# A transformer kernel on one Trainium2 core: GpSimd splits ten more weight units, before and at the start of the sparse attention

## The chip, the core and the metric

The kernel runs on one core of one Trainium2 chip. The engines named here are TensorE (PE in the rows, its weight loads PEld), VectorE (DVE), ScalarE (ACT), GpSimd (POOL) and SyncE (SP, which issues the weight loads). The metric is the device time of one execution in microseconds (us), lower is better. A time is the median of several runs; a profile is one further execution.

## What is computed

The reference is two blocks in fp32 on 256 tokens of width 1024: a first model of two layers (Fourier and window attention, pooling, SwiGLU), and a second block that this change touches. The second block ("third block" in the kernel's own counting, since the first model has two) is, cut to what matters:

```python
h = rmsnorm(x, norm_mix)
(dn_qkv, dn_z, dn_b, dn_a, ns_q, ns_kc, ns_vc, ns_ks, ns_vs, ns_kw, ns_vw, ns_gate,
 gate_dn, gate_nsa) = jnp.split(h @ w_in, splits, axis=-1)
o_dn = gated_deltanet(dn_qkv, dn_z, dn_b, dn_a, ...)
o_ns = nsa_mixer(ns_q, ns_kc, ..., ns_gate, ...)   # compressed, selected and window attention
mix = sigmoid(gate_dn) * (o_dn @ w_proj_dn) + sigmoid(gate_nsa) * (o_ns @ w_proj_nsa)
x = x + mix @ w_out
x = x + square(relu(rmsnorm(x, norm_mlp) @ w_up)) @ w_down
```

The products ns_q, ns_ks, ns_kw and the raw keys and values ns_kc, ns_vc stand first (stage f1 of the kernel), then the token-major values ns_vs, ns_vw (tm1), then dn_qkv (stage f2), beside which the sparse attention runs.

## The kernel before

Every weight product is made of three matmuls of reduced-precision fp32: a weight unit of 128x1024 floats is split into a high part (sb_whi, the rounded copy) and a low part (sb_wlo, weight minus high part), and lines 578 to 580 multiply high by high, high by low and low by high. A unit serves one tile of 128 output features and 24 matmuls. Four pairs of buffers hold split units, so unit n takes the buffers of unit n-4: whoever splits unit n waits until PE has finished unit n-4 and until the unit's chunk has landed (SP loads chunks of two units into ring slots, and reuses a slot when the low parts of its old chunk are done).

Who splits is set by one tuple, POOLED (line 319). For a unit outside it, ACT makes the high part (line 1456) and DVE the low part (line 2039), each at the place in its own queue that the planner `Flow` gives, up to three units ahead of PE's use. For a unit in POOLED, GpSimd makes both parts (lines 2866 and 2868), and PE waits for GpSimd's semaphore s_lo_pool in place of s_lo_dve. Before the change POOLED holds ten units of f2: numbers +5, +7 to +23 counted from f2's first unit.

Counted like that, the units of the stage in question are: -21 to -18, raw keys and values (tiles j = 12 to 15); -17, half a unit, the gates; -16 to -5, queries and keys j = 0 to 11; -4 to -1, values (`values2`); from 0 on, f2. PE runs them in this order, with small products between them. After every odd j from 1 on, `f1_squares(j)` (line 597) sums squares, ACT takes a root (line 1731), DVE inverts it and spreads it over heads (`f1_inverse(j)`, lines 2374 and 2376, the latter a copy of 128x512 within SBUF into sb_tmp), PE turns that (`f1_spread(j)`, line 1031), and DVE scales the tiles with it (`unit_rms(j)`, line 2384). Between them stand the compressed keys and values: DVE writes sb_bk in `blocks(e)` (line 2411, eight tensor-tensor instructions on 64 partitions, two SBUF inputs), PE multiplies it by raw weights (line 1056), DVE and ACT apply a gelu (lines 2417 to 2427, 1764), and PE scores against the result (`cmp_scores`, line 1088), which needs the tiles of `unit_rms(7)`.

No scheduler orders any of this: each engine's queue is the order in which its program function writes it, and engines meet only at semaphores. GpSimd's queue before the change, in this part, is three memsets, then a wait for the end of f1 on PE, ACT and DVE, then per attention step a multiplication of the scores (`weigh`, line 2859) and for every second step a split.

Of the kernel before, what the change touches and what calls it, by code (L numbers as in the profile page):

```python
# [9 lines left out]
ALU = mybir.AluOpType  # L10
# [305 lines left out]

F2 = (*range(8, 16), *range(8), *range(16, 24))
F2_UNIT = FIRST_UNIT[[name for name, _, _, _ in PLAN].index("f2")]
POOLED = tuple(F2_UNIT + s for s in range(5, 24, 2))
ADDED = {"ffn1": 4}  # L320
CUTS = ((0, 128), (128, 384))
NORMS = ("mix0", "ctx", "ffn0", "mix1", "ffn1", "fin", "mix2", "mlp2")
# [9 lines left out]
def program(nc, a):  # L332
    ctx = ExitStack()
    with ctx:
        area = [ctx]

        def sb(name, shape, dt=F32):
            return area[-1].enter_context(nc.sbuf_tensor("sb_" + name, shape, dt))
# [5 lines left out]
        def sem(name):  # L344
            return ctx.enter_context(nc.semaphore(name))
# [12 lines left out]
        pe, act, dve, pool = Mark(sem("s_pe")), Mark(sem("s_act")), Mark(sem("s_dve")), Mark(sem("s_pool"))  # L358
# [100 lines left out]
        ss = sb("ss", [128, 3, 2, 384])  # L459
        pt2 = sb("pt2", [128, 2, 2, 384])  # L460
        nst = st[:, 0:64].rearrange("p (n k u t) -> p n k u t", n=4, k=4, u=2)
# [51 lines left out]
        def landed(c):  # L513
            return s_slot[SLOT_OF[c]], 16 * LOADS[c]

        def unit_of(n):
            c, o, size = UNITS[n]
            return chunk(c)[:, o:o + size], whi[:, n % NUNIT, 0:size], wlo[:, n % NUNIT, 0:size]

        def lo_done(n):  # L520
            return lo_pool.at(n) if n in POOLED else lo_dve.at(n)

# [913 lines left out]
        def scalar_program(sc):  # L1436
# [10 lines left out]
            def split(units):  # L1447

                for n in units:
                    if n in POOLED:  # L1450
                        continue
# [569 lines left out]
        def vector_program(ve):  # L2021
# [10 lines left out]
            def split(units):  # L2032

                for n in units:
                    if n in POOLED:
                        continue
# [762 lines left out]
        def gpsimd_program(gp):  # L2799
            G = Waiter(gp)  # L2800

            def regions(before):

                G.wait_ge(*pe.at(before))
                G.wait_ge(*act.at(before))
                G.wait_ge(*dve.at(before))
# [42 lines left out]
            gp.memset(hvx[:, :, :, :], 0.0).then_inc(*pool.up("hvx"))  # L2849
            gp.memset(bk[:, :, :], 0.0).then_inc(*pool.up("bk"))  # L2850
            gp.memset(pcs[:, :, :, :], 0.0).then_inc(*pool.up("pcs"))
            pool.note("f1")
            regions("f1")
            def weigh(i):
                G.wait_ge(*dve.at("nw", i))
                for t, (lo, hi) in enumerate(CUTS):
                    p = ss[:, i % 3, :, lo:hi]
                    x = nst[:, i % 4, 3, :, t].unsqueeze(2).to_broadcast([128, 2, hi - lo])
                    gp.tensor_tensor(p, p, x, ALU.mult).then_inc(*pool.up(*[("weighed", i)] * t))  # L2859

            def split(n):

                x, hi, lo = unit_of(n)
                G.wait_ge(*landed(UNITS[n][0]))
                G.wait_ge(*pe.at("unit", n - NUNIT))
                gp.tensor_copy(hi, x).then_inc(*pool.up(("hi", n)))
                G.wait_ge(*pool.at("hi", n))
                gp.tensor_tensor(lo, x, hi.bitcast(F32), ALU.subtract).then_inc(*lo_pool.up(n))

            weigh(0)  # L2870
            step = 2
            for s in range(24):
                if STEPS2[s]:
                    if step - 1 < N2:
                        weigh(step - 1)
                    step += 1
                if F2_UNIT + s + AHEAD in POOLED:
                    split(F2_UNIT + s + AHEAD)
# [33 lines left out]
        def sync_program(sp):  # L2912
# [31 lines left out]
            for c in range(len(PLAN)):  # L2944
                if c == 4:
                    sp.dma_start(h[:, :, :], a["xT"]).then_inc(s_x, 16)
                if c == 10:
# [4 lines left out]

        engines = ((tensor_program, nc.tensor), (scalar_program, nc.scalar), (vector_program, nc.vector),
                   (gpsimd_program, nc.gpsimd), (sync_program, nc.sync))
        marks = (pe, act, dve, pool, hi_done, lo_dve, lo_pool)
        for walk, _ in engines:
# [22 lines left out]
        @block.gpsimd  # L2979
        def _(eng):  # L2980
            gpsimd_program(eng)
# [206 lines left out]
```

## Time and profile before

| | us |
|---|---|
| median of 3 runs | 1146.68 (1144.14 to 1146.83) |
| the profiled execution, own time | 1141.37 |
| its span from first to last instruction | 1139.6 |
| PE busy | 1109.6 |
| DVE busy | 812.3 |
| ACT busy | 586.5 |
| POOL busy | 135.4 |

The span is 1.8 us shorter than the execution's own time; what lies around it is not in the trace. PE's busy time is modelled at the ends of matmuls, so small gaps in PE are best read from the list of waits. A wait is written as "who waited, its line <- whose result, its line". In the timeline a row is one or several like instructions, with start, duration, engine, line, operation, and in brackets how long the engine had been idle and what ended that.

### The profile page before, as it was taken

What the parts mean: (1) busy time and instruction counts of PE and PEld (TensorE: products, weight loads), DVE (VectorE), ACT (ScalarE), POOL (GpSimd) and SP (SyncE); (2) the same over time, 40 slices, a digit from 0 to 9 for tenths busy, and PEclk for the clock granted to TensorE, in tenths of its full rate; (3) what the DMA queues carried; (4) which work ended last, traced back from release to release, by engine and by line L of the source; (5) the groups of instructions that cost most, each with busy time, mean ns of one, the idle gap of its engine ahead of it and who ended that gap; (6) DMA issues with size and microseconds to landing.
All of it is one profiled execution on the core that took longest, in us unless ns stands there. A gap on an engine that the chain in (4) does not pass through costs nothing.

```text
span 1139.6 us, 23794 instructions
## 1 busy us (share of the span) xinstructions
PE 1109.6 (97%) x10111; PEld 1049.6 (92%) x10111; DVE 812.3 (71%) x1436; ACT 586.5 (51%) x1081; POOL 135.4 (12%) x143
## 2 busy tenths in 40 slices
PE   8899999999999999999999999999999999999998
PEld 2786889999998999999988888889989999999998
DVE  6887889898887766554766787778545667677553
ACT  2546654545445544554556677653325556565342
POOL 0002100000111000012000365525300002000000
PEclk9899999999999999999999999999999999999999
DMA  9965299898883676540752332322025555755610
GB/s 389 388 249 181 79 365 359 324 337 334 315 344 112 246 279 240 193 163 8 290 185 80 144 112 82 122 94 76 4 74 185 185 186 210 308 188 187 225 55 15
DMA packets 32221, 225.36 MB, mean 198 GB/s; under 512 B 3569, under 2 KB 4721, under 8 KB 5105
## 3 DMA queue, kind: packets, MB, share of 16 engines
q1 hardware_dynamic: 30530, 221.21, 52.0%
q10 hardware_dynamic: 1584, 2.62, 0.7%
q8 instruction: 80, 1.31, 0.5%
q14 instruction: 27, 0.22, 0.1%
HBM read 222.76 MB, written 1.05 MB: 196 GB/s over the span
## 4 chain that ended last, share of the span: by engine, by line
PE 89%; DVE 6%; ACT 3%; DMA 1%; issue 1%; POOL 0%; DVEq 0%; ACTq 0%; POOLq 0%
PE bank L578 24%; PE bank L579 23%; PE bank L580 23%; DVE sb_wlo L2039 2%; PE bank L597 1%; DMA sb_ring<-in_ada 1%; PE bank L1110 1%; PE bank L1141 1%; ACT sb_whi L1456 1%; PE bank L1119 1%; PE bank L1306 1%; PE bank L1324 1%; PE bank L1320 1%; PE bank L673 1%; PE bank L678 1%; PE bank L674 1%
## 5 line engine op out<-in xcount | busy, mean ns | idle before, releaser
L578 PE MATMUL bank<-sb_xh,sb_whi 128*128 128x256 f32 x1480 | 416.7, 282 | 2.5 <-DVE sb_wlo L2039 2.2
L580 PE MATMUL bank<-sb_xh,sb_wlo 128*128 128x256 f32 x1480 | 409.4, 277 | 0.0
L579 PE MATMUL bank<-sb_xl,sb_whi 128*128 128x256 f32 x1480 | 409.4, 277 | 0.0
L2039 DVE TENSOR_TENSOR sb_wlo<-sb_ring,sb_whi 128x1024 fp32r<-128x1024 f32 (+1 forms) x185 | 229.7, 1247 | 103.4 <-ACT sb_whi L1456 103.0
L578 PEld LDWEIGHTS bank<-sb_xh,sb_whi 128*128 128x128 f32 x1480 | 277.7, 188 | 9.5 <-issue 5.6
L579 PEld LDWEIGHTS bank<-sb_xl,sb_whi 128*128 128x128 f32 x1480 | 277.7, 188 | 0.1
L580 PEld LDWEIGHTS bank<-sb_xh,sb_wlo 128*128 128x128 f32 x1480 | 277.5, 188 | 0.0
L1456 ACT ACTIVATE sb_whi<-sb_ring 128x1024 fp32r<-128x1024 f32 (+1 forms) x185 | 194.3, 1054 | 96.7 <-PE bank L580 81.8
L2039 DVE TENSOR_TENSOR sb_wlo<-sb_more,sb_whi 128x1024 fp32r<-128x1024 f32 x110 | 133.9, 1228 | 62.7 <-ACT sb_whi L1456 62.7
L578 PE MATMUL bank<-sb_hh,sb_whi 128*128 128x256 f32 x608 | 168.4, 277 | 0.0
L579 PE MATMUL bank<-sb_hl,sb_whi 128*128 128x256 f32 x608 | 167.8, 276 | 0.0
L580 PE MATMUL bank<-sb_hh,sb_wlo 128*128 128x256 f32 x608 | 167.8, 276 | 0.0
L1456 ACT ACTIVATE sb_whi<-sb_more 128x1024 fp32r<-128x1024 f32 x110 | 116.1, 1058 | 65.8 <-PE bank L580 53.8
L579 PEld LDWEIGHTS bank<-sb_hl,sb_whi 128*128 128x128 f32 x608 | 114.2, 188 | 0.0
L578 PEld LDWEIGHTS bank<-sb_hh,sb_whi 128*128 128x128 f32 x608 | 114.1, 188 | 0.0
L580 PEld LDWEIGHTS bank<-sb_hh,sb_wlo 128*128 128x128 f32 x608 | 114.1, 188 | 0.0
L2814 POOL TENSOR_TENSOR sb_sq<-sb_sq 128x256 f32<-128x256 f32 x22 | 23.9, 1088 | 347.4 <-ACT sb_sq L1478 209.7
L2083 DVE CUSTOM_DVE_ANT_0 sb_ring<-sb_ring,sb_cB,sb_col 128x1024 f32<-128x1024 f32 x44 | 55.6, 1299 | 0.0
L1649 ACT ACTIVATE sb_tmp<-bank 128x256 f32<-128x256 f32 x44 | 16.9, 384 | 66.2 <-PE bank L580 66.2
L2083 DVE CUSTOM_DVE_ANT_0 sb_more<-sb_more,sb_cB,sb_col 128x1024 f32<-128x1024 f32 x36 | 45.4, 1297 | 0.0
L2859 POOL TENSOR_TENSOR sb_ss<-sb_ss,sb_st 128x256 f32<-128x256 f32 (+1 forms) x32 | 26.9, 863 | 134.2 <-DVE sb_st L2507 133.8
L1478 ACT ACTIVATE sb_sq<-sb_h 128x256 f32<-128x256 f32 x40 | 15.8, 414 | 48.4 <-DVE sb_h L2097 43.9
(411 smaller groups left out, 1848.3 us busy)
## 6 DMA issues: line engine op xcount, KB each, us to landing
sb_more<-in_w SPq DMA_DIRECT2D x34, 1024.0 KB, 6.0
sb_ring<-in_w SPq DMA_DIRECT2D x32, 1024.0 KB, 5.9
sb_ring<-in_adaT SPq DMA_DIRECT2D x24, 1024.0 KB, 7.1
sb_ring<-in_f SPq DMA_DIRECT2D x22, 1024.0 KB, 4.9
sb_more<-in_adaT SPq DMA_DIRECT2D x20, 1024.0 KB, 8.5
sb_ring<-in_gn SPq DMA_DIRECT2D x8, 1024.0 KB, 4.8
sb_ring<-in_gd SPq DMA_DIRECT2D x8, 1024.0 KB, 5.0
sb_ring<-in_up SPq DMA_DIRECT2D x8, 1024.0 KB, 8.1
```

Source lines behind the costliest of these rows:

```text
L578: te.matmul(out, wh, rh, start=start, stop=False, skip_group_check=skip)
L579: te.matmul(out, wh, rl, start=False, stop=False, skip_group_check=skip)
L580: return te.matmul(out, wl, rh, start=False, stop=stop, skip_group_check=skip)
L597: end = te.matmul(out(t), src[:, c + t * 128:c + (t + 1) * 128], ones_, start=True, stop=True)
L673: te.matmul(out, hi[:, c], xh[:, k, :], start=clear and k == 0, stop=False, skip_group_check=True)
L1456: sc.activation(hi, x, ACT.Copy).then_inc(*hi_done.up(n))
L1478: sc.activation(sq[:, k, :], src[:, k, :], ACT.Square).then_inc(*act.up(("sq", norm, k)))
L1649: sc.activation(temp(("silu", layer, j), (dve, ("hid", layer, j))), ps_of(("up", layer, j))[:, 0:T], ACT.Silu).then_inc(*act.up(("silu", l ...
L2039: ve.tensor_tensor(lo, x, hi.bitcast(F32), ALU.subtract).then_inc(*lo_dve.up(n))
L2083: ve.tensor_tensor_reduce(out=x, in0=x, in1=cB[:, 0, :], scale=1.0, scalar=C(f"ab{layer}", jj, jj + 1), op0=ALU.mult, op1=ALU.add, accum_o ...
L2814: gp.tensor_tensor(sq[:, 0, :], sq[:, 0, :], sq[:, k, :], ALU.add).then_inc(*pool.up(("sum", norm, k)))
L2859: gp.tensor_tensor(p, p, x, ALU.mult).then_inc(*pool.up(*[("weighed", i)] * t))
```

## The change

POOLED begins 20 numbers earlier: it now holds -15, -13, -11, -9, -7, -5, -3, -1, +1, +3 too, every second unit from there to +23. GpSimd's `split` moves up and is called for the eight units below zero right behind the memsets, ahead of the wait for the end of f1; the split of +1 stands behind that wait and ahead of weigh(0), that of +3 ahead of weigh(1). ACT and DVE each have ten instructions fewer.

```diff
-POOLED = tuple(F2_UNIT + s for s in range(5, 24, 2))
+POOLED = tuple(F2_UNIT + s for s in range(-15, 24, 2))
...
+            def split(n):
+
+                x, hi, lo = unit_of(n)
+                G.wait_ge(*landed(UNITS[n][0]))
+                G.wait_ge(*pe.at("unit", n - NUNIT))
+                gp.tensor_copy(hi, x).then_inc(*pool.up(("hi", n)))
+                G.wait_ge(*pool.at("hi", n))
+                gp.tensor_tensor(lo, x, hi.bitcast(F32), ALU.subtract).then_inc(*lo_pool.up(n))
+
             pool.note("f1")
+            for n in range(F2_UNIT - 15, F2_UNIT, 2):
+                split(n)
             regions("f1")
...
+            split(F2_UNIT + 1)
             weigh(0)
```

GpSimd's queue behind the three memsets, before the change (2859 is weigh, 2866 and 2868 are a split):

```order
L2851 MEMSET sb_pc 128x1024
L2859 TENSOR_TENSOR sb_ss<-sb_ss,sb_st 128x2x128 [waits s_dve,s_act,s_pe]
L2859 TENSOR_TENSOR sb_ss<-sb_ss,sb_st 128x2x256
L2859 TENSOR_TENSOR sb_ss<-sb_ss,sb_st 128x2x128 [waits s_dve]
L2859 TENSOR_TENSOR sb_ss<-sb_ss,sb_st 128x2x256
```

The same place after it (2857 and 2859 are now the split, 2870 is weigh); two of the eight early splits and the last ones before weigh(0):

```order
L2851 MEMSET sb_pc 128x1024
L2857 CAST sb_whi<-sb_ring 128x1024 [waits s_pe,s_slot2]
L2859 TENSOR_TENSOR sb_wlo<-sb_ring,sb_whi 128x1024 [waits s_pool]
L2857 CAST sb_whi<-sb_qk 128x1024 [waits s_pe,s_slot4]
L2859 TENSOR_TENSOR sb_wlo<-sb_qk,sb_whi 128x1024 [waits s_pool]
...
L2857 CAST sb_whi<-sb_ring 128x1024 [waits s_slot2,s_dve,s_pe,s_act]
L2859 TENSOR_TENSOR sb_wlo<-sb_ring,sb_whi 128x1024 [waits s_pool]
L2870 TENSOR_TENSOR sb_ss<-sb_ss,sb_st 128x2x128 [waits s_dve]
```

Eight splits now wait only for PE's progress and the loads, and the ninth (unit +1) has taken over the wait for f1 and stands ahead of weigh(0).

DVE's queue at the start of the stage before the change: the splits of -16, -15, -14 and -13, then blocks(0) (2411), gates (2342 to 2347), the split of -12 and the first head scale (2374, 2376):

```order
L2039 TENSOR_TENSOR sb_wlo<-sb_ring,sb_whi 128x1024 [waits s_hi]
L2337 SCALAR_TENSOR_TENSOR sb_h<-sb_h,sb_col,bank 128x256 x2
L2039 TENSOR_TENSOR sb_wlo<-sb_ring,sb_whi 128x1024 [waits s_hi]
L2337 SCALAR_TENSOR_TENSOR sb_h<-sb_h,sb_col,bank 128x256 x2
L2039 TENSOR_TENSOR sb_wlo<-sb_qk,sb_whi 128x1024 [waits s_hi] x2
L2411 TENSOR_TENSOR sb_bk<-sb_kcv,sb_col 64x16x15 [waits s_act,s_pool]
L2411 TENSOR_TENSOR sb_bk<-sb_kcv,sb_col 64x16x15 x7
```

And after it:

```order
L2039 TENSOR_TENSOR sb_wlo<-sb_ring,sb_whi 128x1024 [waits s_hi]
L2337 SCALAR_TENSOR_TENSOR sb_h<-sb_h,sb_col,bank 128x256 x4
L2039 TENSOR_TENSOR sb_wlo<-sb_qk,sb_whi 128x1024 [waits s_hi]
L2411 TENSOR_TENSOR sb_bk<-sb_kcv,sb_col 64x16x15 [waits s_act,s_pool]
L2411 TENSOR_TENSOR sb_bk<-sb_kcv,sb_col 64x16x15 x7
```

The splits of -15 and -13 have left DVE's queue, and blocks(0) follows the split of -14 with nothing between.

## Rows read from the trace of the kernel before

**Rows 1.** The page: busy us, share and instructions of each engine

```profile
PE 1109.6 (97%) x10111; PEld 1049.6 (92%) x10111; DVE 812.3 (71%) x1436; ACT 586.5 (51%) x1081; POOL 135.4 (12%) x143
```

**Rows 2.** PE's waits, 540 to 760 us: total us, times, longest

```profile
PE bank L597 <- DVE sb_nq L2384: 1.4, 1, 1.4
PE bank L1031 <- DVE sb_tmp L2376: 1.3, 2, 0.9
PE bank L1088 <- DVE sb_hdev L2374: 0.9, 1, 0.9
...
PE bank L578 <- ACT sb_vsw L1812: 0.3, 1, 0.3
```

**Rows 3.** GpSimd's two split instructions: ns minimum/median/maximum, first and last start

```profile
L2866 POOL CAST sb_whi<-sb_ring x10: 1037/1238/1287, 645.7 to 734.1; 128x1024 fp32r<-128x1024 f32 x10
...
L2868 POOL TENSOR_TENSOR sb_wlo<-sb_ring,sb_whi x10: 2357/2372/2446, 647.0 to 735.5; 128x1024 fp32r<-128x1024 f32 x10
```

**Rows 4.** Timeline, GpSimd and DVE beside each other, f2 and behind it

```profile
647.01 2.40 POOL L2868 TENSOR_TENSOR sb_wlo<-sb_ring,sb_whi 128x1024 fp32r<-128x1024 f32 x1
648.64 1.85 DVE L2039 TENSOR_TENSOR sb_wlo<-sb_ring,sb_whi 128x1024 fp32r<-128x1024 f32 x1 [1.06 <-ACT sb_whi L1456]
...
652.37 0.17 DVE L2507 TENSOR_TENSOR sb_st<-sb_st,sb_gate 128x4 f32<-128x4 f32 x1
655.49 2.37 POOL L2868 TENSOR_TENSOR sb_wlo<-sb_ring,sb_whi 128x1024 fp32r<-128x1024 f32 x1
656.19 1.69 DVE L2507 TENSOR_TENSOR sb_st<-sb_st,sb_gate 128x4 f32<-128x4 f32 x1
...
660.26 1.29 POOL L2866 CAST sb_whi<-sb_ring 128x1024 fp32r<-128x1024 f32 x1 [0.69 <-PE bank L580]
660.58 1.25 DVE L2583 SCALAR_TENSOR_TENSOR sb_qk<-sb_tmp,sb_qk 128x256 f32<-128x256 f32 x1
...
759.62 0.34 DVE L2640 TENSOR_SCALAR sb_Msb<-sb_con,sb_gg 128x256 f32<-128x256 f32 x1
759.73 1.09 POOL L2885 TENSOR_TENSOR sb_Msb<-sb_Msb,sb_con 128x384 f32<-128x384 f32 x1 [15.45 <-ACT sb_Msb L1927]
759.88 1.02 DVE L2641 TENSOR_SCALAR sb_Msb<-sb_con,sb_gg 128x128 f32<-128x128 f32 x1
```

**Rows 5.** Timeline, start of the queries: ACT, DVE, PE, 558 to 571 us

```profile
558.32 0.38 ACT L1711 ACTIVATE sb_tmp<-bank 64x256 f32<-64x256 f32 x1 [0.44 <-PE bank L580]
...
558.89 1.22 DVE L2039 TENSOR_TENSOR sb_wlo<-sb_qk,sb_whi 128x1024 fp32r<-128x1024 f32 x1
...
562.68 1.23 DVE L2039 TENSOR_TENSOR sb_wlo<-sb_qk,sb_whi 128x1024 fp32r<-128x1024 f32 x1 [2.58 <-ACT sb_whi L1456]
563.82 4.09 DVE L2411 TENSOR_TENSOR sb_bk<-sb_kcv,sb_col 64x240 f32<-64x240 f32 x8
...
569.93 0.43 DVE L2376 COPY sb_tmp<-sb_hdev 128x512 f32<-128x512 f32 x1
...
570.47 0.60 PE L1031 MATMUL bank<-sb_con,sb_tmp 128*128 128x128 f32 x4
```

**Rows 6.** Timeline, end of f1 and the values: PE, DVE, ACT, 602 to 634 us

```profile
602.49 0.60 PE L1031 MATMUL bank<-sb_con,sb_tmp 128*128 128x128 f32 x4
...
605.32 1.23 DVE L2039 TENSOR_TENSOR sb_wlo<-sb_ring,sb_whi 128x1024 fp32r<-128x1024 f32 x1 [1.05 <-ACT sb_whi L1456]
...
612.21 0.60 PE L1031 MATMUL bank<-sb_con,sb_tmp 128*128 128x128 f32 x4
...
614.05 1.23 DVE L2039 TENSOR_TENSOR sb_wlo<-sb_ring,sb_whi 128x1024 fp32r<-128x1024 f32 x1 [2.67 <-ACT sb_whi L1456]
...
626.77 0.25 DVE L2481 TENSOR_TENSOR sb_cst<-sb_cst,sb_gate 128x8 f32<-128x8 f32 x2
...
633.17 0.66 ACT L1812 ACTIVATE sb_vsw<-bank 128x256 f32<-128x256 f32 x2 [0.59 <-PE bank L580]
```

**Rows 7.** PE by 2 us stretches: length, PE busy (instructions), granted clock, DMA share, GB/s

```profile
618.00:620.00 2.00, 1.61 (x8) 0.50 0.00 0
```

More of the change, by code:

```diff
@@ L2859, in weigh @@
                     gp.tensor_tensor(p, p, x, ALU.mult).then_inc(*pool.up(*[("weighed", i)] * t))
[L2861 to L2868, printed above, removed]
+            split(F2_UNIT + 1)
             weigh(0)
```

## The prediction

> **What bounds the kernel now.** The page first: PE is busy for 1109.6 of 1139.6 us [rows 1], so nothing that makes DVE or ACT idle more is worth anything unless PE waits for it. The list of PE's waits for the stretch of the change comes next. From 540 to 760 us the waits that end in this part's work are four kinds [rows 2]: 1.4 us at line 597 for the bank that unit_rms(3) frees, 1.3 us in two waits at line 1031 for the head scale of line 2376 (0.9 the longer), 0.9 us at line 1088 for unit_rms(7) (its second instruction ends just ahead of the one named), and 0.3 us at line 578 for ACT's copy of the values. That is 3.9 us in all, and it is the ceiling of what relief can give before any clock is counted. PE never waits there for a split. In f2 itself, where GpSimd splits already, no row of the list names DVE or ACT work behind a split, so the four later places decide.
>
> **What the relief is worth.** Ten ACT and ten DVE instructions go, about 1.05 and 1.22 us each. Only those on the way to one of the four waits count. Unit -9's low part stands ahead of the gelu that leads to the 1.4 us wait: 1.1 us off it. Unit -5's parts stand ahead of the second gelu, which leads through ACT's split of -4 to the 0.9 us wait; the next limit on that way (ACT must wait for PE's tile j = 9) is about 0.95 us earlier than now, so this wait would go. The other places (0.5, 0.9 and 0.3 us) hang on work that stays. Relief alone: about -2.0 us.
>
> **What a GpSimd split costs.** A cast of 1.04 to 1.29 us and a subtraction of 2.36 to 2.45 us [rows 3], 3.5 us with the gap, against one in 5.6 us of PE's time. GpSimd has nothing else to do there. PE's own need of these units is covered: unit n's buffers are free three units (8 us and more) before it is wanted, and 3.5 us is less. Unit -15 is wanted at 561.2, and its buffers are free three units before, near 552.8 [rows 5]. The loads are issued when low parts are done, and those come earlier, not later. weigh(0), now behind the split of +1, moves by a few us, and PE turns its scores only two attention steps later. All of that costs nothing.
>
> **What the split does to DVE.** In [rows 4] DVE's subtraction of line 2507, 128x4, takes 0.17 us at 652.37 and 1.69 us at 656.19; the second ends at 657.88, where GpSimd's subtraction of 655.49 ends (657.86). Line 2039 begins at 648.64 under a GpSimd subtraction that ends at 649.41, and ends 1.22 us after about 649.27. So a DVE instruction with two SBUF inputs does not run beside GpSimd's; it waits for its end. A fast one-input operation within SBUF does as well: line 2641 takes 1.02 us at 759.88 beside GpSimd's 759.73. Who comes next is seen there too: DVE's 2640 runs to 759.96, 2641 is queued right behind it, and GpSimd, which asked at 759.73, gets in between. So does the cast of 660.26 ahead of DVE's 2583, which begins at 660.58 and ends at 661.83, 0.28 us behind the cast. I take it that they alternate: each lets the other's waiting instruction go after its own current one.
>
> The Trainium skill has this as a rule (SBUF — State Buffer, section "Who interferes with whom"): the pair of ports that DVE and GpSimd share is an exclusive lock held for the whole instruction, and a DVE instruction with two SBUF inputs contends with a GpSimd one that reads SBUF. The rows agree to 0.1 us. A reader who takes instead the mean lengthening of line 2039's rows (some 0.5 us on 1.22) as a slowdown in proportion gets the second rival below.
>
> **Term 1, the start.** On the clock of before [rows 5]. PE ends the gates' unit -17 at 558.2 (ACT takes it at 558.32) and j = 3, unit -13, at 570.5, where line 1031 starts. Between them are four units of 2.8 us and 1.1 us of small work, so -15 ends at 564.0. Hence the casts of -13, -11 and -9 are released at 558.3, 564.1 and 570.6. DVE reaches the split of -14 at 558.7, waits for the cast of -13 (559.4) and ends it at 560.6. GpSimd's subtraction then holds DVE until 562.9, where blocks(0) starts; that is 0.9 us earlier than now (563.82). Two or three of its eight instructions (0.51 us each) pass by 564.4, then the cast of -11 (to 565.4), one more, then its subtraction (565.9 to 568.3), then the rest: blocks(0) ends at 570.4 and not at 567.9. From its end to that of line 2376 it is 2.45 us now (567.91 to 570.36), with two small two-input instructions and one of line 2039. The cast of -9 is released at 570.6, and its subtraction ends at 574.2; the split of -12 comes behind it, then 2374 and 2376: 576.1. PE wants it at 570.5. The stall is 5.6 us. If DVE kept the port through a run of queued instructions, I get 573.3, a stall of 2.7 us; if they shared it freely, none. I take 5.6, since the rows at 660.26 and 759.73 show GpSimd getting in.
>
> **Term 2, the first gelu.** After the stall blocks(1) runs with GpSimd idle. The 0.5 us wait at the second line 1031 goes. The gelu and the split of -8 meet the split of -7 (released when j = 5 ends), and the wait at line 597 stays at about 1.3 us in place of 0.3. Net -0.5 us.
>
> **Term 3, unit_rms(7).** [Rows 6], again on the clock of before: -3's split is released when j = 9 ends, at 602.5, and holds until 606.2. ACT's high part of -4 would let line 2039 start 0.95 us earlier, at 604.4; it gets the port at 606.15 and not at 605.32 as now. +0.85 us at line 1088.
>
> **Term 4, head scale 11.** Unit -1's split runs from 612.4 (j = 11 ended at 612.2) to 616.0. Line 2039 for -2, at 614.05 now, starts at 615.9, and everything to line 2376 and PE follows: +1.85 us.
>
> **Term 5, the values.** Unit +1's split runs from 626.1 to 629.6. It holds line 2481 at 626.77 and what follows; the scores of pair 1 and their exponentials come 2.5 us late. ACT has one cast less (1.0 us) and idles 0.6 us ahead of its copy at 633.17, so PE's first f2 unit waits 0.9 us longer.
>
> **Clock.** Behind the present stall at 618 the granted clock is 0.50 for a stretch of 2 us [rows 7], the lower level of 1.2 GHz; the engine had done little but small matmuls and waits before. A stall of 5.6 us at 570.5 should bring the same: 2 us at half speed lose 1.0 us; bounds 0 and 2.
>
> Sum: 5.6 - 0.5 + 0.85 + 1.85 + 0.9 + 1.0 = +9.7 us. The profiled execution took 1141.37 us, of which 1139.6 are span, so one like it would take 1151.1; the median of the runs is 1146.68, 5.3 above it, and becomes **1156.4**.
>
> **The rivals.**
> *GpSimd gets in less (2.7 in place of 5.6, no clock loss):* 2.7 - 0.5 + 0.85 + 1.85 + 0.9 = +5.8, 1152.5. For it: a run of eight queued instructions is not in the rows.
> *Slowed in proportion:* each DVE instruction that meets a split loses some 0.5 us. Four or five of them before 570.5 eat 2.3 us of the 3.3 us by which blocks(0) could start earlier (563.82 against 560.6), and no stall appears; later four meetings on the way to waits cost 2.0 and the relief gives 2.0: 0, 1146.7. Against it: 1.69 us for 128x4 elements.
> *Relief wins, not slower:* if the 64-partition instructions of line 2411 pass beside GpSimd, blocks(0) ends near 565, line 2376 at 568 at the latest, and the later meetings fall into DVE's idle time: -2.0, 1144.7. It decides at one point, whether line 2376 is done by 570.5. For it: DVE is idle for 2.58 us ahead of 562.68. To be faster by more, the clock loss at 618 would have to go too (another 1 to 1.4 us with its wait), which hangs on ACT's and DVE's split of -2, and those stay.
> *The change doesn't do what it says:* GpSimd held by a late load, and PE waiting for s_lo_pool. The cover is 4.5 us, so this is small, and it counts with the slower ones.
>
> **Chances.** Forecast 0.50, less getting in 0.15, late splits 0.02: slower by over 0.3% 0.67. Proportion 0.14 and relief 0.14: within 0.3% (3.4 us, about what a measurement of this kernel tells from no change) 0.28. Faster by more 0.05. The range starts at relief's value, less 0.2, and ends 3.6 above the forecast, for a clock loss of 2 and another 2.6 us where ties between the engines fall badly: 1144.5 to 1160. Below it lies some 0.1, above some 0.1.
>
> **What would show it.** In the profile after: PE's first line 1031 in f1 waits for line 2376 by about 5.6 us (2.7 in the first rival, 0 in the others); DVE's line 2411 x8 takes 7 to 8 us and not 4.09; small two-input DVE instructions of 1 to 2 us beside GpSimd's subtraction; the waits at 1088 and at the last 1031 near 1.7 and 2.7 us; granted clock of 0.5 behind the first stall. If line 2411 still takes 4.1 us with a GpSimd split over it, term 1 falls, and the time is near 1145.

## The result and the profile after

The changed kernel takes **1152.7 us** (median of 8 runs, 1146.29 to 1155.0) against 1146.76 for the kernel before (8 runs, 1143.75 to 1147.41): a ratio of 1.0049, 95% interval 1.0025 to 1.0073, or 3 to 8 us slower. The forecast was 1156.4, the range 1144.5 to 1160. The same kernel in a later comparison gave 1.0035 (1.0013 to 1.0057), so +4 to +6 us is what the change costs. The profiled execution took 1151.45 us.

The head of its page: the span, then busy time, share and instructions of each engine ([rows 1] before).

```profile
span 1149.7 us, 23806 instructions
PE 1115.7 (97%) x10111; PEld 1054.8 (92%) x10111; DVE 820.6 (71%) x1426; ACT 577.2 (50%) x1071; POOL 172.7 (15%) x163
```

Ten instructions left DVE, some 12 us of work, and DVE is busy for 8.3 us longer than before. Its instructions wait inside their own duration. The page's group of line 2039 (count, busy us and mean ns, then the idle time ahead) shows it; before, the mean was 1247 ns over 185 instructions.

```profile
L2039 DVE TENSOR_TENSOR sb_wlo<-sb_ring,sb_whi 128x1024 fp32r<-128x1024 f32 (+1 forms) x177 | 230.0, 1304 | 105.9 <-ACT sb_whi L1456 105.5
```

PE's waits of the changed kernel, 540 to 775 us: who waited for whom, total us, times, longest ([rows 2] before).

```profile
PE bank L1269 <- DVE sb_Msb L2641: 2.1, 1, 2.1
PE bank L1031 <- DVE sb_tmp L2376: 1.9, 1, 1.9
PE bank L1110 <- DVE sb_pc L2462: 1.7, 1, 1.7
PE bank L1088 <- DVE sb_hdev L2374: 1.7, 1, 1.7
PE bank L597 <- DVE sb_nq L2384: 1.5, 1, 1.5
PE bank L578 <- ACT sb_vsw L1812: 1.4, 1, 1.4
PE bank L1073 <- ACT sb_hx L1768: 0.3, 1, 0.3
...
```

Without the first row, which lies at 760 us, and the 0.2 of line 673, which is there before and after, they come to 8.5 us. Before they were 4.5 (the 3.9 of [rows 2], and 0.3 us each at lines 606 and 1073). No wait for s_lo_pool is among them: GpSimd's splits are never late.

The rest of the difference between these two profiles is TensorE's clock. PE by stretches, the changed kernel: length, PE busy (instructions), granted clock, DMA share, GB/s.

```profile
536.00:544.00 8.00, 7.43 (x54) 1.00 0.58 213
584.00:596.00 12.00, 10.16 (x104) 0.86 0.07 18
604.00:616.00 12.00, 10.31 (x80) 0.72 0.25 87
616.00:628.00 12.00, 10.12 (x89) 0.85 0.25 89
756.00:772.00 16.00, 13.90 (x96) 0.89 0.26 95
```

The same stretches of the kernel before:

```profile
536.00:544.00 8.00, 7.51 (x40) 0.79 0.46 169
584.00:596.00 12.00, 10.33 (x119) 1.00 0.34 106
604.00:616.00 12.00, 11.14 (x129) 1.00 0.46 167
616.00:628.00 12.00, 11.12 (x84) 0.86 0.16 48
756.00:772.00 16.00, 14.25 (x103) 1.00 0.19 67
```

A granted clock of 0.86 over 12 us is a stretch at 0.50, the level of 1.2 GHz, that loses 12 x 0.14 = 1.7 us. Five such losses stand against two, 8.6 us against 3.4: +5.2. With +4.0 of waits and +0.4 at line 1269 that is 9.6 of the 10.1 us between the spans (1149.7 and 1139.6). Only the waits can be laid to the change at once. The profiled execution of before was quicker than each of its 8 runs (5.4 us under their median), that of after is 1.3 under its own median, so a part of the 5.2 us is the luck of two executions. How large that part is, the clocks of all runs show (the table under "Which units are worth it").

### The profile page after: what moved, and what is told of

It reads as the page before. It is cut to its first block, busy times and chain, and to the rows that moved or that the text cites. A ratio compares the mean times of both kernels' runs of the same rounds, so it can differ in the third digit from the quotient of the medians.

```text
span 1149.7 us, 23806 instructions
## 1 busy us (share of the span) xinstructions
PE 1115.7 (97%) x10111; PEld 1054.8 (92%) x10111; DVE 820.6 (71%) x1426; ACT 577.2 (50%) x1071; POOL 172.7 (15%) x163
## 3 DMA queue, kind: packets, MB, share of 16 engines
HBM read 222.76 MB, written 1.05 MB: 195 GB/s over the span
## 4 chain that ended last, share of the span: by engine, by line
PE 88%; DVE 8%; ACT 3%; issue 1%; POOL 0%; DMA 0%; ACTq 0%; DVEq 0%; POOLq 0%
PE bank L578 23%; PE bank L580 22%; PE bank L579 22%; DVE sb_wlo L2039 3%; PE bank L702 1%; PE bank L597 1%; PE bank L1141 1%; PE bank L1110 1%; ACT sb_whi L1456 1%; PE bank L1119 1%; PE bank L1306 1%; PE bank L1324 1%; PE bank L1320 1%; PE bank L673 1%; DVE sb_bk L2411 1%; PE bank L678 1%
## 5 line engine op out<-in xcount | busy, mean ns | idle before, releaser
L1456 ACT ACTIVATE sb_whi<-sb_ring 128x1024 fp32r<-128x1024 f32 (+1 forms) x177 | 185.9, 1053 | 96.4 <-PE bank L580 82.4
L2859 POOL TENSOR_TENSOR sb_wlo<-sb_ring,sb_whi 128x1024 fp32r<-128x1024 f32 x18 | 44.4, 2469 | 1.4
```

Source lines behind the costliest of these rows:

```text
L1456: sc.activation(hi, x, ACT.Copy).then_inc(*hi_done.up(n))
```

## The experiments

All are compared with the kernel before in 5 rounds. The forecast's theory, called the port theory in the expectations, is that GpSimd's reads hold DVE, and that DVE's lateness reaches PE. Against it stand three others: that GpSimd's splits come late, that the clock alone costs, or that any added work on GpSimd does. In each version GpSimd's calls of `split` follow the tuple.

### One half of the change at a time

Only the eight units below zero:

```diff
-POOLED = tuple(F2_UNIT + s for s in range(5, 24, 2))
+POOLED = tuple(F2_UNIT + s for s in (-15, -13, -11, -9, -7, -5, -3, -1, *range(5, 24, 2)))
```

> The changed kernel with +1 and +3 given back to ACT and DVE; GpSimd keeps the eight splits of -15 to -1. Port theory: the waits of PE before the values stay as in the changed kernel (line 1031 about 1.9, line 597 about 1.5, line 1088 about 1.7, line 1110 about 1.7 us), the wait for ACT's copy of the values falls from 1.4 back to 0.3 us; time 1.1 us below the changed kernel's 1152.7, about 1151.5. Rival, late splits (what costs is that weigh(0) and f2 stand behind +1 and +3): most of the 6 us go, 1147.

Measured: 1147.25 against 1144.59, ratio 1.0032 (1.0014 to 1.005). The rival's 1147 is met in microseconds, but only because the kernel before ran 2.2 us quicker in this comparison; as a ratio the rival says 1.000 and the port theory 1.004, and the measured one rules the first out. The waits are those of the changed kernel, without the one for the values (0.3 at line 578), with 0.5 in place of 1.7 at line 1110, which was not expected, and with the 0.3 at line 606 that the kernel before has too.

The other two units, +1 and +3:

```diff
-POOLED = tuple(F2_UNIT + s for s in range(5, 24, 2))
+POOLED = tuple(F2_UNIT + s for s in range(1, 24, 2))
```

> The kernel before with only +1 and +3 added to GpSimd; nothing in f1 changes. Port theory: PE's wait at line 578 for ACT's copy of the values grows from 0.3 to 1.2 to 1.4 us, f1's waits stay at 3.6 us in all; time 1147.7 (+1.0, within the noise of the kernel before). Rival, late splits: +4 to +6, 1151 to 1153.

Measured: 1145.9, ratio 1.0008 (0.9988 to 1.0027), as the port theory had it. In the list of waits the one at line 578 for ACT's copy is 1.4 us as in the changed kernel (0.3 before); the 0.3 at line 606 is gone, and the others are those of before to 0.1 us. So these two splits make the wait for the values, 1.1 us, and the early eight make all the others.

The 0.5 us at line 1110 in the first of these runs is a lesson in reading. Its timeline, PE and DVE:

```profile
615.38 0.60 PE L1031 MATMUL bank<-sb_con,sb_tmp 128*128 128x128 f32 x4
...
619.04 1.95 PE L1078 MATMUL bank<-sb_col,sb_hvx 128*128 128x64 f32 x8
...
620.93 0.46 DVE L2462 TENSOR_TENSOR sb_pc<-bank,sb_con 128x120 f32<-128x120 f32 x2
...
621.54 1.65 PE L1110 MATMUL bank<-sb_ksw,sb_nq 64*128 64x128 f32 x8 [0.55 <-DVE sb_pc L2462]
```

and that of the changed kernel:

```profile
616.93 0.60 PE L1031 MATMUL bank<-sb_con,sb_tmp 128*128 128x128 f32 x4
...
618.34 2.35 POOL L2859 TENSOR_TENSOR sb_wlo<-sb_ring,sb_whi 128x1024 fp32r<-128x1024 f32 x1
618.76 3.01 DVE L2039 TENSOR_TENSOR sb_wlo<-sb_ring,sb_whi 128x1024 fp32r<-128x1024 f32 x1 [4.58 <-ACT sb_whi L1456]
620.26 1.08 PE L1078 MATMUL bank<-sb_col,sb_hvx 128*128 128x64 f32 x8
...
623.08 1.66 PE L1110 MATMUL bank<-sb_ksw,sb_nq 64*128 64x128 f32 x8 [1.74 <-DVE sb_pc L2462]
...
624.40 0.43 DVE L2376 COPY sb_tmp<-sb_hdev 128x512 f32<-128x512 f32 x1
...
624.89 1.12 PE L1031 MATMUL bank<-sb_con,sb_tmp 128*128 128x128 f32 x4
```

and PE of the kernel before, behind the 612.21 of [rows 6]:

```profile
616.59 0.93 PE L1110 MATMUL bank<-sb_ksw,sb_nq 64*128 64x128 f32 x8
...
618.39 1.12 PE L1031 MATMUL bank<-sb_con,sb_tmp 128*128 128x128 f32 x4 [0.88 <-DVE sb_tmp L2376]
```

From line 1031 to line 1110 it is 6.2 us in both of the first (4.38 before). In the first, PE ran line 1078 in 1.95 us, at a granted clock of 0.50 (619 to 621 us); in the changed kernel it takes 1.08 at 1.00 (620 to 622 us). Its slow matmuls filled the wait (the rest of the difference is line 597, 1.38 us for 1.05). The changed kernel does the same one step on: line 1110 takes 1.66 us there (0.51 granted from 623 to 625 us) and 0.93 before, and line 1031 follows line 2376 without a wait, while the whole way from line 1031 to the next line 1031 has grown from 6.18 to 7.96 us. DVE sets these times; the list of waits shows only what PE has left of them.

### Is it the reading, or the work?

GpSimd is given as much work at the same places, but writes only: four memsets of the same buffers, 3.4 us. The split of these ten units is left out, and constants stand in for their weights. So PE multiplies other numbers; whether that touches its clock is not shown, but DVE's durations below do not hang on it.

```diff
+                if n < F2_UNIT + 5:
+                    gp.memset(hi.bitcast(F32), 0.03125).then_inc(*pool.up(("hi", n)))
+                    G.wait_ge(*pool.at("hi", n))
+                    gp.memset(lo.bitcast(F32), 0.0).then_inc(*pool.up())
...
+                    gp.memset(lo.bitcast(F32)[:, 0:512], 0.0).then_inc(*pool.up())
...
+                    gp.memset(lo.bitcast(F32), 0.0).then_inc(*lo_pool.up(n))
+                    return
```

> The changed kernel, but for the ten added units GpSimd fills the high and low parts with constants (memsets of about the same length, 0.95 and 2.4 us) and reads no weight, so these products are of constants; ACT and DVE are relieved as in the changed kernel. Port theory (it is GpSimd's reading of SBUF that holds DVE's two-input instructions): line 2411 x8 back to 4.1 us, PE's first wait at 1031 gone, the waits at 597 and 1088 at 0.3 and 0 us, time 1144.7, up to 3.4 lower by clock stretches that go, 1141 to 1146. Rival (GpSimd's length, its place in the chain of semaphores or any GpSimd access is what costs): 1150 to 1153 as the changed kernel.

The other way round: the kernel before, with ACT and DVE splitting all, and GpSimd reading beside them. It copies and subtracts at the eight early places, and nobody uses what it writes. (It writes as well as reads; that writing costs nothing is what the first of the two runs tests.)

```diff
+            for n in range(F2_UNIT - 15, F2_UNIT, 2):
+                x, y = flat(xh[:, 0:4, :]).bitcast(F32), flat(sq[:, 4:8, :])
...
+                G.wait_ge(*landed(UNITS[n][0]))
+                G.wait_ge(*pe.at("unit", n - NUNIT))
+                gp.tensor_copy(y, x).then_inc(*pool.up(("x", n)))
+                G.wait_ge(*pool.at("x", n))
+                gp.tensor_tensor(y, x, y, ALU.subtract).then_inc(*pool.up(("y", n)))
```

> The kernel before, all splits where they were, but GpSimd also runs eight pairs of a copy and a two-input subtraction of 128x1024 (activations read, a free part of sb_sq written, nobody uses it), released as the splits of -15 to -1 are in the changed kernel. Port theory: the cost without the relief, so more than the changed kernel: 2 us more waiting, +8 (6 to 12), 1152 to 1158, line 2411 x8 at 7 to 9 us. Rival (moving the splits away from ACT and DVE, or PE's waits for GpSimd's semaphore, is what costs): same as before, 1146.8.

Measured: writes only 1140.9, ratio 0.9973 (0.9958 to 0.9989); reads only 1154.13, ratio 1.0095 (1.007 to 1.012). The longest waits of the first:

```profile
PE bank L597 <- DVE sb_nq L2384: 0.7, 1, 0.7
PE bank L1031 <- DVE sb_hx L2417: 0.4, 1, 0.4
```

and of the second:

```profile
PE bank L1031 <- DVE sb_tmp L2376: 5.7, 2, 5.5
PE bank L1088 <- DVE sb_hdev L2374: 2.2, 1, 2.2
PE bank L1110 <- DVE sb_pc L2462: 1.8, 1, 1.8
```

One DVE group tells the two apart at its source, the eight two-input instructions of line 2411. In the timeline of writes only it takes what it took before ([rows 5], 4.09 us), with GpSimd writing beside it (one memset of four is shown; they run from 556.68 to 560.25):

```profile
556.52 4.10 DVE L2411 TENSOR_TENSOR sb_bk<-sb_kcv,sb_col 64x240 f32<-64x240 f32 x8
```

```profile
557.69 0.96 POOL L2860 MEMSET sb_wlo<- 128x1024 f32 x1
```

With reads only it takes 6.88 us (7 to 9 expected):

```profile
562.44 6.88 DVE L2411 TENSOR_TENSOR sb_bk<-sb_kcv,sb_col 64x240 f32<-64x240 f32 x8
```

So the reads cost, not the work: the relief alone is worth 3.1 us, the reads alone cost 10.9. The two do not add up to the change's 5.6: the first covers ten units and the second eight, and DVE stands elsewhere when GpSimd asks. The Trainium skill (SBUF — State Buffer, section "Who interferes with whom") says that a DVE instruction with two SBUF inputs contends with a GpSimd one that reads SBUF and not with one that only writes it; 4.10 beside the memsets and 6.88 beside the copies agree.

### Shorter turns

The ten added splits in four pieces each, 128x256:

```diff
+                if n < F2_UNIT + 5:
+                    for q in range(4):
+                        c = slice(q * 256, (q + 1) * 256)
+                        gp.tensor_copy(hi[:, c], x[:, c]).then_inc(*pool.up(*[("hi", n)] * (q == 3)))
...
+                        end = gp.tensor_tensor(lo[:, c], x[:, c], hi[:, c].bitcast(F32), ALU.subtract)
...
```

> The changed kernel, each of the ten added casts and subtractions in four pieces of 128x256. GpSimd's work grows (about 0.3 and 0.7 us a piece, 4 us a split), but no piece holds the port for more than 0.7 us. Port theory, with turns taken after each instruction: a DVE instruction waits for one piece and not for a whole subtraction, so the waits at 597, 1088, 1110 fall to some 0.7, 1.1 and 1.0 us, the first at 1031 stays between 0 and 2; ratio to before about 1.001 (0.999 to 1.003) against the changed kernel's 1.0049. Rival (the port is divided by time share, so the total GpSimd time counts, not the length of a piece): 1.005 or more.

Measured: 1147.12 against 1145.65, ratio 1.0013 (0.9998 to 1.0028). The groups of the pieces (count, busy us and mean ns):

```profile
L2864 POOL TENSOR_TENSOR sb_wlo<-sb_ring,sb_whi 128x256 fp32r<-128x256 f32 x32 | 28.5, 921 | 0.6
L2860 POOL CAST sb_whi<-sb_ring 128x256 fp32r<-128x256 f32 x32 | 13.4, 459 | 36.2 <-PE bank L580 36.2
```

A split costs GpSimd 4 x (0.92 + 0.46) = 5.5 us in place of 3.5, and yet PE's waits fall from 8.5 to 2.6 us, since a DVE instruction now waits for a turn of about 0.9 us and not for 2.4. The eight of line 2411 show it (ns, minimum, median and longest, of one), here and in the changed kernel:

```profile
L2411 DVE TENSOR_TENSOR sb_bk<-sb_kcv,sb_col x8: 579/820/1033, 556.8 to 562.0; 64x240 f32<-64x240 f32 x8
```

```profile
L2411 DVE TENSOR_TENSOR sb_bk<-sb_kcv,sb_col x8: 558/564/2687, 558.0 to 566.4; 64x240 f32<-64x240 f32 x8
```

The lock is handed over at instructions. The time does not fall as far as the waits. In this profile the clock accounts for that: 0.93 granted between 540 and 640 us, where the kernel before has 0.97, so 4 us lost. Over all runs it accounts for little (+0.7 us in the table below), and why the time stays at that of before with 1.9 us less waiting isn't shown.

### Which units are worth it

If relief counts only where a unit stands ahead of a wait, a few units should do, and those that hold DVE should be left.

```diff
-POOLED = tuple(F2_UNIT + s for s in range(5, 24, 2))
+POOLED = tuple(F2_UNIT + s for s in (-9, -5, *range(5, 24, 2)))
```

> The kernel before, with only units -9 and -5 added to GpSimd: the two whose DVE part stands ahead of a gelu that PE waits for, and whose GpSimd split runs while DVE has slack. Port theory: wait at 597 from 1.4 to 0.7 or less, at 1088 from 0.9 to 0, the others as before; ratio 0.9985 (0.997 to 1.000). Rival (any split on GpSimd in f1 costs): 1.001 or more.

The same with `(-9, -4, -2, *range(5, 24, 2))`:

> The kernel before, with -9, -4 and -2 added to GpSimd: the last two are the units whose split stands right ahead of unit_rms(7) and unit_rms(9) on DVE. Port theory: waits at 597 0.7 or less, at 1088 0, at the last 1031 (head scale 11) 0 in place of 0.9, a new one of up to 0.3 at 1031 for head scale 7 (GpSimd's subtraction of -4 runs until 602.3 on the clock of before); with the low-clock stretch at 618 gone too, ratio 0.996 (0.9945 to 0.999). Rival (any split on GpSimd in f1 costs): 1.001 or more.

The changed kernel without -13 and -11, `(-15, -9, -7, -5, -3, -1, *range(1, 24, 2))`, to test the first stall alone:

> The changed kernel with -13 and -11 given back to ACT and DVE, so that no GpSimd split runs over blocks(0). Port theory: line 2411 x8 back to 4.1 us, PE's first wait at 1031 (1.9 us) gone, the waits at 597, 1088, 1110 and 578 stay at 1.5, 1.7, 1.7 and 1.4; ratio 1.003 (1.0015 to 1.005). Rival (the stall at 1031 comes from the backlog of earlier splits, not from the overlap with line 2411): the 1.9 us stay, 1.005.

Measured: 0.9964 (0.9951 to 0.9978) with -9 and -5, quicker than the whole range expected; 0.9959 (0.9944 to 0.9973) with -9, -4 and -2; 1.0041 (1.0026 to 1.0057) without -13 and -11. In the last, line 2411 takes its 4.13 us again and the first wait for line 2376 is gone; 0.7 us for line 2417 and 0.9 for line 2427, the gelus behind it, come in its place. Line 1110 waits 0.6 us and not the 1.7 expected; here too line 1078 runs in 1.95 us and fills it. The first stall is therefore not what the time hangs on.

Then both picks together, and the changed kernel beside it once more:

```diff
-POOLED = tuple(F2_UNIT + s for s in range(5, 24, 2))
+POOLED = tuple(F2_UNIT + s for s in (-9, -5, -4, -2, *range(5, 24, 2)))
```

> The kernel before with -9, -5, -4 and -2 added to GpSimd, the two selections that were faster together. Both take the wait at 1088 away already (0.9 us), so only -5's part ahead of the second gelu could still give something, and that wait is gone: port theory expects no gain over -9, -4, -2 alone, ratio 0.996 (0.9945 to 0.9975). Rival (each unit taken off ACT and DVE is worth its share, some 0.2% for two): 0.994.

> The changed kernel once more, on the chip and in the rounds of this job. PE's six waits of the stretch come back to 0.1 us (1.9 at 1031, 1.5 at 597, 1.7 at 1088, 1.7 at 1110, 1.4 at 578, 2.1 or 1.7 at 1269), since they follow from order and durations alone. If the number of stretches at the low clock is a matter of chance, it differs from the first profile's (588, 608 to 616, 620 to 627, 764 us) and the time with it, 1.7 us a stretch; ratio 1.005 (1.003 to 1.008).

Measured: **1138.47** against 1144.66, ratio 0.9948 (0.9929 to 0.9968), the fastest version; the changed kernel 1147.61, ratio 1.0035. Three units gave 0.9959, so what the fourth adds isn't told apart; the rival's 0.994 lies within the interval too. PE's waits with four units:

```profile
PE bank L1031 <- DVE sb_hx L2417: 0.9, 2, 0.7
PE bank L597 <- DVE sb_nq L2384: 0.3, 1, 0.3
PE bank L578 <- ACT sb_vsw L1812: 0.3, 1, 0.3
```

GpSimd's turns do not fall into DVE's idle time there. They hold DVE as before, line 2376 twice by 2.1 us (0.43 alone) and line 2039 once by 1.8, but at places where PE does not need the result yet, or waits 0.2 us. The second of the two copies:

```profile
606.20 2.55 DVE L2376 COPY sb_tmp<-sb_hdev 128x512 f32<-128x512 f32 x1
```

The second profile of the changed kernel has the waits of its first to within 0.2 us, and its low stretches of the clock elsewhere: 0.72 from 584 to 596 us (0.86 in the first), 1.00 from 756 to 772 us (0.89). The waits belong to the kernel; where the clock falls differs between executions, though not everywhere: line 1110, behind its wait of 1.7 us, runs at the low level in both (1.66 and 1.65 us).

All of them, with PE's waits between 540 and 760 us in the profile (line 673's 0.2 left out; before: 4.5 us), and the time against before from the ratio. The last two columns take the time apart over all runs. Each run has its span and its mean granted clock, and (1 - clock) x span is an estimate of what its low stretches cost: in 31 runs of the kernel before, the spans scatter by 1.9 us (standard deviation), and by 0.8 once this is taken off. The columns are differences of means, so they do not add up exactly to the time by the ratio; the rest is known to within 1 us.

| version | waits, us | against before | time against before, us (95%) | of it clock (95%) | the rest |
|---|---|---|---|---|---|
| -9, -5, -4, -2 | 1.8 | -2.7 | -6.0 (-8.1 to -3.7) | -4.1 (-5.9 to -2.3) | -1.1 |
| -9, -4, -2 | 1.7 | -2.8 | -4.7 (-6.4 to -3.1) | -3.7 (-5.1 to -2.2) | -1.1 |
| -9, -5 | 2.5 | -2.0 | -4.1 (-5.6 to -2.5) | -2.9 (-4.0 to -1.7) | -1.3 |
| writes only | 1.7 | -2.8 | -3.1 (-4.8 to -1.3) | -1.4 (-3.0 to +0.2) | -1.7 |
| only +1, +3 | 5.4 | +0.9 | +0.9 (-1.4 to +3.1) | -0.1 (-2.2 to +2.0) | +0.6 |
| quarters | 2.6 | -1.9 | +1.5 (-0.2 to +3.2) | +0.7 (-0.9 to +2.1) | +0.4 |
| early eight | 6.6 | +2.1 | +3.7 (+1.6 to +5.7) | +0.4 (-1.1 to +1.9) | +2.9 |
| without -13, -11 | 7.2 | +2.7 | +4.7 (+3.0 to +6.5) | +0.3 (-1.2 to +1.6) | +4.3 |
| the change | 8.5 | +4.0 | +5.6 (+2.9 to +8.4) | clocks of before not on record | |
| the change again | 8.4 | +3.9 | +4.0 (+1.5 to +6.5) | -0.8 (-2.8 to +1.4) | +4.7 |
| reads only | 11.9 | +7.4 | +10.9 (+8.0 to +13.7) | +2.9 (+0.6 to +5.5) | +7.2 |

But for the quarters the order of the times is that of the waits, within their intervals. In the slower versions the cost lies in the rest, which is near the waits; only with reads only has the clock a part that is clear of zero. Where the rest is larger than the waits, a part of the surplus is waits that slow matmuls fill (about 1 us in the change, the early eight and the one without -13 and -11).

In the faster versions it is the other way round. With two, three and four chosen units over two thirds of the gain is clock: low stretches that the kernel before has and they have less of. What brings them and takes them away isn't shown. It isn't the sum of the waits alone, since writes only has as few of them as three or four chosen units and gains less clock, and the quarters gain none.

## The prediction, point by point

- **What bounds the kernel**: right. Four waits, 3.9 us, were the ceiling of the relief before any clock (-2.0 us forecast). Writes only gave -3.1 (-4.8 to -1.3), waits down by 2.8. The chosen units go beyond that ceiling (-6.0), and do it by the clock, which the prediction priced at 1 to 1.4 us and tied to the split of -2; -9 and -5 without it gain 2.9 us of clock too.
- **What a GpSimd split costs** GpSimd and PE: right. No wait for s_lo_pool; late splits fall as a rival, and so does "the change doesn't do what it says".
- **What the split does to DVE**: right, including that GpSimd gets in between queued instructions. It is the step on which the forecast rests. Slowing in proportion falls: of the eight instructions of line 2411 five take 0.56 us as before and three 2.69, 1.20 and 2.64 (the median is 564 ns, the longest 2687), and the time would have been unchanged. That the 64-partition instructions pass beside GpSimd falls by the same number.
- **Term 1** is the step that failed, in size: 5.6 us forecast, 1.90 measured. The timeline of the changed kernel at this place:

```profile
557.04 3.33 POOL L2859 TENSOR_TENSOR sb_wlo<-sb_qk,sb_whi 128x1024 fp32r<-128x1024 f32 x1
558.03 8.92 DVE L2411 TENSOR_TENSOR sb_bk<-sb_kcv,sb_col 64x240 f32<-64x240 f32 x8
561.86 1.19 POOL L2857 CAST sb_whi<-sb_ring 128x1024 fp32r<-128x1024 f32 x1 [1.49 <-PE bank L580]
563.12 2.48 POOL L2859 TENSOR_TENSOR sb_wlo<-sb_ring,sb_whi 128x1024 fp32r<-128x1024 f32 x1
...
567.60 1.22 DVE L2039 TENSOR_TENSOR sb_wlo<-sb_ring,sb_whi 128x1024 fp32r<-128x1024 f32 x1
568.29 1.42 POOL L2857 CAST sb_whi<-sb_ring 128x1024 fp32r<-128x1024 f32 x1 [2.69 <-PE bank L580]
...
568.97 1.03 DVE L2376 COPY sb_tmp<-sb_hdev 128x512 f32<-128x512 f32 x1
569.80 2.43 POOL L2859 TENSOR_TENSOR sb_wlo<-sb_ring,sb_whi 128x1024 fp32r<-128x1024 f32 x1
569.92 3.38 DVE L2039 TENSOR_TENSOR sb_wlo<-sb_ring,sb_whi 128x1024 fp32r<-128x1024 f32 x1
570.05 0.66 PE L1031 MATMUL bank<-sb_con,sb_tmp 128*128 128x128 f32 x4 [1.90 <-DVE sb_tmp L2376]
```

  This kernel is 2.47 us ahead of the clock of before here (the first matmul behind line 1011 starts at 558.72, before at 561.19). Line 2411 ends at 566.95, on that clock 569.4, where the forecast had 570.4. The 8.92 us hold 2.3 in which its first instruction waits for GpSimd's subtraction (to 560.37); from there the eight take 6.6 us, and the forecast's own working has 7.5 (562.9 to 570.4), since four of them pass ahead of the next cast and not two or three. That 1 us decides: the split of -12 starts at 567.60, ahead of the cast of -9 (released 568.29), and line 2376 waits only for this cast (1.03 us instead of 0.43). The forecast had the subtraction come ahead of it too; in the changed kernel it holds the next line 2039 (3.38 us), which PE does not wait for. With reads only, where DVE still has its own splits to do, the race is lost (the split of -12 starts at 570.32, GpSimd's subtraction at 570.25) and PE waits 5.5 us. So the mechanism was right, and a race that was decided by 0.7 us was read as certain.
- **Term 2**, -0.5: the second wait at line 1031 is gone (0.46), line 597 has 1.5 us for 1.4. Right.
- **Term 3**, +0.85 at line 1088: 1.7 for 0.9. Right.
- **Term 4**, +1.85 up to head scale 11: +1.78 (7.96 us for 6.18), but the wait stands one matmul group earlier, at line 1110, whose bank line 2462 frees; line 2039 takes 3.01 us as it waits for the subtraction of -1.
- **Term 5**, +0.9 at the values: +1.1, in the change and with +1 and +3 alone.
- **Clock**, +1.0: none behind the first stall, where the granted clock is 1.00 from 566 to 580 us; that stall was 1.9 us and not 5.6. With reads only, behind a stall of 5.5 us, it is 0.50 from 574 to 578 us and 0.65 in the 2 us behind, a loss of 2.7 us. Over the profiled pair the clock costs some +5. Over the runs of the later comparison it is -0.8 (-2.8 to +1.4), so nothing that can be told from none.
- **The sum**: +9.7 forecast. The terms as measured are 1.9 - 0.5 + 0.85 + 1.8 + 1.1 = +5.1; the list of waits shows 1.1 less, 0.9 of it filled by the slow line 1110 and 0.3 a wait at line 606 that is gone. Over the runs of the later comparison the change costs +4.7 us (3.9 to 5.7) outside the clock, which the 5.1 of the terms meets. By the ratios the time moved by +5.6 (2.9 to 8.4) and +4.0 (1.5 to 6.5). The forecast is 3.7 us above the median of 1152.7, the size of term 1's error, and that this one difference closes the sum is luck: the terms as measured give 5.1, no low clock follows the first stall, and by the later comparison the forecast is 5.7 us too high. That the median of 1152.7 is near the first rival's 1152.5 does not speak for it: its stall was to be 2.7 us because DVE keeps the port through a run, and DVE doesn't.

## What to carry to other kernels

Handing work from DVE to GpSimd does not relieve DVE where it stands behind the handed work with two-input or fast copy instructions: count GpSimd's reading time as DVE's, at the place where the two meet. Hand over only units that stand on DVE's way to a wait, and whose GpSimd turn holds DVE only where PE does not need its next result yet; here four such units gain 0.5%, over two thirds of it by a clock that falls less often, where ten cost 0.4 to 0.5%. That the way to a wait is what makes them good was not tested against four units picked otherwise. A test that swaps reads for writes, and one that adds reads without relief, separate the two effects in two runs.

## What was not expected

- The lock goes by turns even within a run of queued instructions: line 2411, eight instructions of 0.51 us, is held at its start, broken up twice and takes 8.92 us.
- A wait in PE's list can be filled by PE's own slow clock (line 1078, 1.95 us for 1.08); the interval between two fixed points, 6.2 us in both, is the safer reading.
- The clock's low stretches move between executions of one kernel with the same waits, at about 1.7 us each: in the later comparison the runs of the changed kernel spread from 1144.2 to 1153.6 us, and those of the kernel before from 1138.9 to 1148.5.
- Cutting a GpSimd split in four makes it 2 us longer, and PE's waits 6 us shorter.
